# Side work of a recurrent mixer placed at later points of the matmul stream

## The reference, cut to what matters

```python
f = lb + (1.0 - lb) * jax.nn.sigmoid(hg_heads(f_h))
o_hg = hgrn2_chunked(jax.nn.silu(hg_heads(q_h)), jnp.log(f), 1.0 - f, hg_heads(i_h))
o_hg = o_hg * lax.rsqrt(jnp.mean(o_hg * o_hg, axis=-1, keepdims=True) + RMS_EPS) * hg_norm_w[l]
o_hg = o_hg * jax.nn.silu(hg_heads(g_h))
```

## Time and profile before

| | |
|---|---|
| time, median of 3 runs | 2327.02 us (2325.89 to 2327.72) |
| profiled execution | 2318.02 us |
| its span, slowest core | 2316.4 us (cores: 2308.7 to 2316.4 us) |
| PE busy in the span | 2219.8 us (96%) |
| DVE, ACT, POOL busy | 804.0, 563.3, 236.6 us |
| mean granted TensorE clock, slowest core | 0.988 |

### The profile page before, as it was taken

The page is one execution under the profiler, slowest core; times in us unless marked ns, Lnnn a source line. Parts: engine busy times, 40 slices in busy tenths (PEclk is TensorE's granted clock), DMA queues, the critical chain, the costliest instruction groups (busy, mean ns, idle before and its releaser), DMA issues.

```text
span 2316.4 us, 36005 instructions; the slowest of 8 cores (2308.7 to 2316.4 us)
## 1 busy us (share of the span) xinstructions
PE 2219.8 (96%) x14656; PEld 1190.8 (51%) x14656; DVE 804.0 (35%) x1287; ACT 563.3 (24%) x939; POOL 236.6 (10%) x217
## 2 busy tenths in 40 slices
PE   3999999999999999999999979999999999999998
PEld 2676766766655554444444534444444444444443
DVE  3443322245544543111112453044134224314416
ACT  4432111144554553111112553000000000000014
POOL 1000000001010112221210000000000000000000
PEclk9999999999999999999999989999999999999999
DMA  9965574231532507756596517655655655555533
GB/s 225 188 130 74 74 92 56 27 48 14 61 48 27 70 1 134 89 66 84 73 186 84 91 19 99 83 78 75 83 80 75 83 74 73 73 73 75 75 51 146
DMA packets 242097, 188.73 MB, mean 81 GB/s; under 512 B 3472, under 2 KB 228752, under 8 KB 237968
## 3 DMA queue, kind: packets, MB, share of 16 engines
q0 software_dynamic: 234448, 145.01, 49.3%
q1 hardware_dynamic: 7488, 41.43, 5.1%
HBM read 323.04 MB, written 8.39 MB: 143 GB/s over the span
## 4 chain that ended last, share of the span: by engine, by line
PE 89%; DVE 4%; ACT 2%; DMA 2%; issue 1%; DVEq 0%; another core or an unknown queue 0%; POOL 0%; ACTq 0%; POOLq 0%
PE P L304 88%; DMA wb<-w_in 2%; DVE hU L880 1%; DVE R L789 1%; DVE R L878 1%; DVE R L820 1%; PE P L1070 1%; PE P L369 1%; ACT R L785 0%; ACT L785 0%; ACT R L818 0%; DVE R L783 0%; PE P L843 0%; DVE R L1060 0%; DVE R L1035 0%
## 5 line engine op out<-in xcount | busy, mean ns | idle before, releaser
L304 PE MATMUL P<-hT,wb 128*128 128x512 bf16 (+1 forms) x6016 | 1342.8, 381 | 19.1 <-DMA wb<-w_in 12.4
L304 PEld LDWEIGHTS P<-hT,wb 128*128 128x128 bf16 x6016 | 582.9, 98 | 692.4 <-issue 36.6
L304 PE MATMUL P<-wb,hT 128*128 128x128 bf16 (+1 forms) x6464 | 716.5, 271 | 7.4 <-DVE R L315 3.2
L304 PEld LDWEIGHTS P<-wb,hT 128*128 128x128 bf16 x6464 | 461.5, 108 | 259.5 <-issue 10.5
L1035 DVE TENSOR_TENSOR R<-R,P 128x512 f32<-128x512 f32 x384 | 262.8, 686 | 144.2 <-PE P L304 144.0
L1245 DVE TENSOR_TENSOR hT<-P,tmp 128x512 bf16<-128x512 f32 x88 | 60.8, 691 | 543.1 <-PE P L304 543.1
L1244 ACT ACTIVATE tmp<-P 128x512 f32<-128x512 f32 x88 | 52.5, 597 | 780.0 <-PE P L304 779.9
L283 POOL DMA_DIRECT2D wb<-w x66 | 65.7, 996 | 889.5 <-PE P L304 882.2
L991 DVE TENSOR_TENSOR tmp<-P,R 128x512 f32<-128x512 f32 x64 | 44.2, 691 | 246.2 <-PE P L304 246.2
L975 ACT ACTIVATE R<-P 128x512 f32<-128x512 f32 x64 | 38.2, 597 | 249.7 <-PE P L304 249.7
L283 POOL DMA_DIRECT2D wb<-w_in x50 | 57.6, 1164 | 394.7 <-PE P L304 394.7
(11 more groups left out here) (116 smaller groups left out, 996.3 us busy)
## 6 DMA issues: line engine op xcount, KB each, us to landing
wb<-w POOLq DMA_DIRECT2D x66, 1024.0 KB, 13.6
wb<-w_in POOLq DMA_DIRECT2D x50, 1024.0 KB, 17.7
R<-xo SPq DMA_DIRECT2D x16, 1024.0 KB, 10.1
R<-xp SPq DMA_DIRECT2D x8, 1024.0 KB, 9.2
wb<-w_out POOLq DMA_DIRECT2D x8, 1024.0 KB, 20.0
y<-R SPq DMA_DIRECT2D x14, 512.0 KB, 2.8
wb<-wkv_c POOLq DMA_DIRECT2D x4, 1024.0 KB, 17.8
wb<-w_bb POOLq DMA_DIRECT2D x8, 512.0 KB, 10.0
```

The source lines that it names most:

```text
L304: P.pe(lambda e: e.matmul(out, lhsT, rhs, start=start, stop=stop, skip_group_check=skip), reads=reads, writes=writes)
```

## The change

The three points of a former half's side work in the next unit go from 3.0, 4.5 and 6.0 to 6.0, 7.5 and 9.0, and the point of the mean square in every unit but the first from 2.6 to 3.5. Nothing else is changed, and the same instructions are issued.

```diff
-        HG_AT = {0: (5.7, 7.0, 12.2), 1: (3.0, 4.5, 6.0), 2: (5.7, 7.0, 12.2)}
+        HG_AT = {0: (5.7, 7.0, 12.2), 1: (6.0, 7.5, 9.0), 2: (5.7, 7.0, 12.2)}
...
-                weave(hg_dense(u, Wp), [(t, 1, prev) for t in HG_AT[u % 3]] + [(2.6, 0, old)], None)
+                weave(hg_dense(u, Wp), [(t, 1, prev) for t in HG_AT[u % 3]] + [(3.5, 0, old)], None)
```

## The result

The changed kernel takes 2299.76 us (median of four runs), the one before 2326.45 us beside it: 26.7 us less, ratio 0.988 with a 95% interval of 0.9866 to 0.9893. The sum of the prediction was -30.5 us. The profiled execution of the fourth experiment ran at a lower clock on cores 4 to 7, so of it only cores 0 to 3 are read.

A forecast was written before the change was run, and what follows sets the result against it. TensorE's recurrent-stage waits, chiefly for the former half's key-side product, and the slow clock after them were taken as the bound; -20.6 - 13.6 + 3.7 = -30.5 us against the 2327.02 us median gave 2296.5 us, range 2291 to 2311.

The forecast's parts named there:

- (a): Unit after a former half: later transposes and state product fill TensorE's waiting with 12 matmuls, 20.6 us saved.
- (b): Behind the transposes of all eight heads: granted clock no longer falls, 13.6 us saved, bounds 0 to 13.6.
- (c): Mean square one step later in the units after former halves: its own wait goes, already counted in the waiting saved.
- (d): Former-half units: mean-square copy falls behind tanh and table load, scores wait 0.53 us in seven units, 3.7 us added.
- (e): DVE and ACT queues that the moved steps pass: delays covered, ACT's second transposes copy fitting by a hair.
- rival 4: State copy blocks DVE ahead of the next unit's gate work; at 7 us lateness +10, 2337 us; chance 0.04.
- Rival 1: Remaining half microsecond of waiting before the transposes still brings the clock down in every head: -16.9, 2310 us; chance 0.09.
- rival 2: ACT held up at the former-half units' table switch, scores wait 2.1 us instead of 0.53: -19.6, 2307 us; chance 0.05.
- rival 3: Key-side product `kl` slips as much as the transposes, waits and slow clock stay: +3.7, 2330.7 us; chance 0.05.

The follow-up runs named there:

- fourth experiment: Mean square at 3.5 in all units as in the change, former half's points left at 3.0, 4.5, 6.0; against the kernel before: ratio 1.0028, 6.5 us slower.
- fifth experiment: Changed kernel with former half's points only one step later than before (4.3, 5.2, 7.0), mean square at 2.6; ratio 0.9912 to the kernel before.
- seventh experiment: Changed kernel with points at 7.0, 8.7, 10.5 and mean square back at 2.6 in former-half units; ratio 0.9849 to the kernel before.
- third experiment: Changed kernel with the mean square back at 2.6 in former-half units only; ratio 0.9857 to the kernel before, 33.3 us less.
- experiment 5: Changed kernel with former half's points only one step later than before (4.3, 5.2, 7.0), mean square at 2.6; 20.5 us under the kernel before.

## Why the prediction was right

The forecast of 2296.5 us is 3.3 us under the median measured, inside the range, and the stage of core 3, from which its terms were read, lost 30.9 us against a sum of 30.5. That the two agree so closely is in part the choice of the core: the other stages lost 25.6 to 30.8 us, and the time is that of whichever core is last.

- **(a) Waiting, 20.6 us.** Confirmed. The two rows of waits lost 18.7 + 5.0 - 2.9 - 0.7 = 20.1 us. About half a microsecond stayed in front of the transposes, as reckoned. The prediction took all eight waits for the square as heads; the eighth is the stage's end, which changes nothing in its sum of seven heads and the first.
- **(b) The clock, 13.6 us.** Confirmed on core 3, where the lost clock went from 13.6 us to 0.0. The fifth experiment separates it from (a). 13.6 us is the most that any core lost, and the upper bound of this term: core 1 lost as much, the other six 8.5 to 12.0 us, since 54 of the 64 heads fell and not all.
- **(c)** Confirmed: the mean square waits for nothing in those units.
- **(d) The new wait, 3.7 us.** Confirmed: 0.50 us against 0.53 in the unit shown; without it the stage is 3.0 us shorter. The tanh starts 0.01 us behind the end of its table load (573.21 + 1.28); the drain that the Trainium skill states ("ScalarE: Activation LUTs", section What ACT_TABLE_LOAD costs) would, by the estimate in (d), have made each wait 1.9 us, and no run here shows it.
- **(e) Queues.** The state product at 548.58 waits for nothing, and the third projection neither; ACT's second copy, which was to fit by a hair, ended at 548.01. One cover was too large, without effect at the change's own points: I gave line 783 the time of ACT's table load as well. The load waits with the logarithm behind it (0.68 us in the seventh experiment, then 1.28 us of load), so the cover was about 0.6 us and not 1.9, and by its own sum rival 4 would have decided from 0.6 + 30.5/8 = 4.4 us of lateness instead of 5.7.

Rival 1 falls with the clock of after, which stays at 1.00 behind all transposes, rival 2 with the wait of 0.34 us for line 894, rival 3 with `kl`, which stayed where it was in the unit. Rival 4's mechanism is real: its first waits come with points one step behind those chosen.

## What to carry to other kernels

Price a wait of TensorE together with the clock of the stretch behind it: here 2.3 us of waiting cost 1.7 us more afterwards in most heads, and the first 0.87 us taken off it brought back all of that. When side work is moved to a later point, follow each evacuation in its own engine's order; an unchanged copy that slips behind an activation and its table load was the only thing that the change made worse. And of two waits in a row, removing the first one alone gained nothing here (fourth experiment).

## What the runs showed that was not expected

PE sometimes idles for no releaser that the profile shows. Of 28 such idles over 0.5 us in the stages of these profiles, 20 are in unit 6, a former half in which four weight blocks are being loaded, each before the last 14 matmuls of a tile of its value projection; six are in unit 7 and two elsewhere. Core 4 of the changed kernel and core 0 of the third experiment, PE's timeline, and the granted clock behind each:

```profile
582.48 1.02 PE L304 MATMUL P<-wb,hT 128*128 128x128 bf16 x14 [1.99 <-issue]
```

```profile
582.00:584.00 2.00, 1.30 (x15) 1.12 (x16) 1.89 (x2) 1.91 (x4) 0.00 (x0) 0.80 1.39 184
584.00:586.00 2.00, 2.00 (x6) 0.75 (x5) 1.30 (x3) 1.35 (x2) 0.60 (x1) 0.50 1.57 136
```

```profile
576.22 0.94 PE L304 MATMUL P<-wb,hT 128*128 128x128 bf16 x14 [2.07 <-issue]
```

```profile
576.00:578.00 2.00, 1.73 (x18) 1.27 (x19) 1.89 (x2) 1.76 (x4) 0.00 (x0) 1.00 1.50 195
578.00:580.00 2.00, 2.00 (x11) 0.88 (x9) 1.30 (x3) 1.15 (x1) 0.95 (x1) 1.00 1.28 139
```

The kernel before has it too (0.63 to 0.97 us on three cores), so it is not the change's. An idle of 1.99 us brought the clock down on one core and one of 2.07 us did not on another. With the waits of up to 1.8 us of experiment 5 it fell in none of 64 heads. In the kernel before it fell in 54 of the 62 heads with waits of 2.15 to 2.66 us: all eight of core 3, five of the eight of core 6. So the length of one idle alone doesn't decide it; what else does was not tried, and neither was the cause of the idle.
